# Both heads of an attention job in turn, block by block, with the causal mask added on VectorE

## What is computed

```python
# branch a: 12 query heads of 64 in 4 key groups, window of 128, ALiBi bias, sinks
scores = jnp.where(valid, q @ k.T * d**-0.5 + bias, NEG)        # a block of 128 queries sees 256 keys
m = jnp.maximum(jnp.max(scores), sink)
p = jnp.exp(scores - m);  denom = jnp.sum(p) + jnp.exp(sink - m)
# branch b ("forgetting"): 12 heads of 64, causal over all 512 tokens
sc = q @ k.T * scale + cq[..., None] - c[:, :, None, :]
sc = jnp.where(key_pos <= qpos, sc, NEG);  p = jax.nn.softmax(sc)
# branch c: 4 heads of 128 over 256 memory tokens, no mask
sc = q @ mk.T * d**-0.5;  p = jax.nn.softmax(sc)
out = p @ v                                                      # in all three
```

## Time and profile before

| | |
|---|---|
| median of 3 runs | 2411.13 us |
| profiled execution, span from first to last instruction | 2409.1 us |
| TensorE products busy | 2273.2 us (94%), 10216 instructions |
| TensorE weight loads busy | 1830.8 us (76%) |
| VectorE busy | 1176.2 us (49%) |
| ScalarE busy | 803.9 us (33%) |
| GpSimd busy | 255.5 us (11%) |
| mean granted TensorE clock | 0.975 of full speed |

### The profile page before, as it was taken

The page is one execution under the profiler, slowest core; times in us unless marked ns, Lnnn a source line. Parts: engine busy times, 40 slices in busy tenths (PEclk is TensorE's granted clock), DMA queues, the critical chain, the costliest instruction groups (busy, mean ns, idle before and its releaser), DMA issues.

```text
span 2409.1 us, 32542 instructions
## 1 busy us (share of the span) xinstructions
PE 2273.2 (94%) x10216; PEld 1830.8 (76%) x10216; DVE 1176.2 (49%) x2028; ACT 803.9 (33%) x1515; POOL 255.5 (11%) x243
## 2 busy tenths in 40 slices
PE   3669999989996899999999999999999999999999
PEld 1457888868775777777777778888888888888887
DVE  4985445566766654444455555543333333334432
ACT  3123222233334334444444444522222222223221
POOL 0860000002220121111001011100000000000000
PEclk8789999999997999999999999999999999999999
DMA  8652333355552432222221222233232333332443
GB/s 354 230 224 70 96 96 96 96 184 189 188 198 81 136 118 78 78 78 78 70 79 61 76 65 90 83 98 96 96 96 96 96 97 99 97 97 89 140 149 113
DMA packets 75822, 280.22 MB, mean 116 GB/s; under 512 B 8677, under 2 KB 11493, under 8 KB 68337
## 3 DMA queue, kind: packets, MB, share of 16 engines
q1 hardware_dynamic: 67872, 259.40, 32.7%
q10 hardware_dynamic: 4848, 10.62, 1.1%
q0 software_dynamic: 3040, 9.46, 1.1%
HBM read 269.98 MB, written 9.46 MB: 116 GB/s over the span
## 4 chain that ended last, share of the span: by engine, by line
PE 81%; DVE 6%; issue 4%; DVEq 3%; DMA 3%; ACT 2%; ACTq 1%; SPq 0%; POOL 0%; POOLq 0%
PE bank L361 25%; PE bank L363 24%; PE bank L362 24%; PE bank L451 3%; PE bank L481 2%; DMA x<-x_features 2%; DVE w_lo L355 1%; PE bank L465 1%; ACT w_hi L345 1%; PE bank L489 1%; DMA w_raw<-stream 1%; DVE h_raw L1196 1%; DVE x_lo L1201 1%; DVE wmod L1172 0%; DVE mod L1177 0%
## 5 line engine op out<-in xcount | busy, mean ns | idle before, releaser
L361 PE MATMUL bank<-x_hi,w_hi 128*128 128x512 f32 x2896 | 1158.0, 400 | 71.0 <-DVE x_lo L1201 53.7
L362 PE MATMUL bank<-x_lo,w_hi 128*128 128x512 f32 x2896 | 1133.3, 391 | 0.0
L363 PE MATMUL bank<-x_hi,w_lo 128*128 128x512 f32 x2896 | 1132.8, 391 | 0.0
L355 DVE TENSOR_TENSOR w_lo<-w_raw,w_hi 128x512 fp32r<-128x512 f32 x724 | 507.2, 701 | 1067.8 <-ACT w_hi L345 1041.6
L345 ACT ACTIVATE w_hi<-w_raw 128x512 fp32r<-128x512 f32 x724 | 457.4, 632 | 1194.8 <-PE bank L363 1096.6
L361 PEld LDWEIGHTS bank<-x_hi,w_hi 128*128 128x128 f32 x2896 | 547.3, 189 | 206.8 <-DVE x_lo L1201 55.8
L363 PEld LDWEIGHTS bank<-x_hi,w_lo 128*128 128x128 f32 x2896 | 546.8, 189 | 116.9
L362 PEld LDWEIGHTS bank<-x_lo,w_hi 128*128 128x128 f32 x2896 | 547.4, 189 | 114.8 <-issue 5.7
L733 POOL TENSOR_TENSOR probs<-probs,rden 128x128 f32<-128x128 f32 (+2 forms) x112 | 80.3, 746 | 547.4 <-DVE rden L644 547.4
L549 ACT ACTIVATE probs<-probs,neg_max 128x128 f32<-128x128 f32 (+2 forms) x112 | 57.8, 517 | 90.3 <-DVE neg_max L632 90.0
L1503 POOL TENSOR_TENSOR w_lo<-front_raw,w_hi 128x512 fp32r<-128x512 f32 x32 | 77.6, 2446 | 32.6 <-ACT w_hi L345 32.6
(11 more groups left out here) (146 smaller groups left out, 1254.8 us busy)
## 6 DMA issues: line engine op xcount, KB each, us to landing
w_raw<-stream SPq DMA_DIRECT2D x362, 512.0 KB, 3.8
wmod<-w_mod_rows SPq DMA_DIRECT2D x48, 1024.0 KB, 6.5
front_raw<-stream SPq DMA_DIRECT2D x8, 1024.0 KB, 8.4
x<-x_features ACTq DMA_DIRECT2D x4, 1024.0 KB, 21.5
x_in<-x_features SPq DMA_DIRECT2D x16, 256.0 KB, 6.6
x_store<-tmp POOLq DMA_DIRECT2D x16, 256.0 KB, 3.5
x_back<-x_store SPq DMA_DIRECT2D x16, 256.0 KB, 4.5
result_features<-result ACTq DMA_DIRECT2D x16, 256.0 KB, 4.3
```

The lines of the kernel that those rows point to most:

```text
L355: nc.vector.tensor_tensor(w_lo[:, q, :], raw_quarter(s), w_hi[:, q, :].bitcast(F32), ALU.subtract).then_inc(lo_ready, 1)
L361: nc.tensor.matmul(bank_ap[:, :tokens], hi, x_hi[:, kx, :], start=start, stop=False)
L362: nc.tensor.matmul(bank_ap[:, :tokens], hi, x_lo[:, kx, :], start=False, stop=False)
L363: return nc.tensor.matmul(bank_ap[:, :tokens], lo, x_hi[:, kx, :], start=False, stop=stop)
```

## The change

- The causal mask is no longer a product on TensorE. `causal` is kept as fp32, and `dve_scores` adds it on VectorE to the 128 columns of neg_c that belong to the diagonal of the block, for both heads, before the scores of that block are read. The bf16 identity and mask and their copies at the start go.
- Scores, exponentials, scaling, transposes and values go by a running number k over both heads. `block_of` gives head and block: head k % 2, block k // 2 in a, and the largest block first in b. Banks alternate by k % 2. A pair (2p, 2p + 1) is the same block of both heads.
- Scores of pair p stand before quarter p + 1, transposes of pair p before quarter p + 4 (two heads) or p + 5 (one head, as before). All values of a two-head job stand behind quarter 7, with the heads alternating inside each key block. In c they stay before quarter 7.
- The denominator is made per pair, one beat behind the exponentials. The sink exponential in a is made per block (one column) instead of per head (four columns).

```diff
+                self.pairs = 2 * self.heads
+                self.base = self.head.times(4)
+                self.turn_beat = 4 if self.heads == 2 else 5
+        def block_of(kind, k):
+            if kind == "c":
+                return 0, k
+            return k % 2, NB - 1 - k // 2 if kind == "b" else k // 2
...
+        def pe_scores(pe, at, p):
...
+            for k in (2 * p, 2 * p + 1):
+                slot, n = block_of(at.kind, k)
+                rows, width, k0 = rows_of(at.kind, slot), LEN[at.kind][n], KEY0[at.kind][n]
+                pe.wait_ge(score_read, (at.base + k + ONE).value())
+                nc.tensor.matmul(score[k % 2][:, :width], q_t[rows, n * P:(n + 1) * P],
+                                 k_t[rows, k0:k0 + width], start=True, stop=True).then_inc(score_full, 1)
-                if at.kind == "b":
-                    mm = nc.tensor.matmul(score[n % 2][:, width - P:width], ident_b[:, :], causal_b[:, :],
-                                          start=False, stop=True, skip_group_check=True)
...
+        def pe_turn(pe, at, p):
+            for k in (2 * p, 2 * p + 1):
+                slot, n = block_of(at.kind, k)
+                pe.wait_ge(probs_ready, (at.base + (k + 1)).value())
+                pe.wait_ge(turned_copied, (at.base + k + ONE).value())
...
+        def pe_values(pe, at):
...
+            for p in range(NB):
+                ks = [p] if at.heads == 1 else [2 * p, 2 * p + 1]
+                pe.wait_ge(turned_copied, (at.base + (ks[-1] + 2) + ONE).value())
+                n = block_of(at.kind, ks[0])[1]
                 count = LEN[at.kind][n] // P
                 for kb in range(count):
                     o = OFF[at.kind][n] + kb * P
+                    for slot in range(at.heads):
+                        rows = rows_of(at.kind, slot)
+                        mm = nc.tensor.matmul(ctx_out[rows, n * P:(n + 1) * P], v_n[:, KEY0[at.kind][n] // P + kb, rows],
+                                              probs_t[:, slot, o:o + P], start=kb == 0, stop=kb == count - 1)
...
+            def before(beat):
+                if at and 1 <= beat <= at.pairs:
+                    pe_scores(pe, at, beat - 1)
+                if beat == 2 and w.prev == "v":
                     pe_turn_values(pe, msrc, T, w.misc_n)
+                if at and 0 <= beat - at.turn_beat < at.pairs:
+                    pe_turn(pe, at, beat - at.turn_beat)
+                if beat == 6 and w.first != "gate":
                     pe_squares(pe, msrc, ones if w.first == "qc" else blocks, T, w.misc_n + (w.prev == "v"))
+                if beat == 7 and at and at.kind == "c":
+                    pe_values(pe, at)
...
+            if at and at.kind != "c":
+                pe_values(pe, at)
...
+                if at.kind == "a":
+                    nc.scalar.activation(sink_exp[:, k:k + 1], neg_max[:, k:k + 1], ACT.Exp,
+                                         bias=sink_col[:, slot:slot + 1]).then_inc(sink_done, 1)
...
+                if at and 1 <= s <= at.pairs:
+                    act_exp(act, at, s - 1)
                 if s == 4 and w.first != "gate":
...
+                if at and 0 <= s - at.turn_beat < at.pairs:
+                    act_turned(act, at, s - at.turn_beat)
...
+        def dve_scores(dve, at, p):
             dve.drain()
+            if at.kind == "b":
+                n = block_of("b", 2 * p)[1]
+                for slot in range(2):
+                    if p == 0:
+                        dve.wait_ge(neg_c_loaded[slot], (at.job + 1).times(16).value())
+                    seg = neg_c[:, slot, n * P:(n + 1) * P]
+                    nc.vector.tensor_tensor(seg, seg, causal[:, :], ALU.add)
+                dve.drain()
...
+                if at and 2 <= s < 2 + at.pairs:
+                    dve_denominator(dve, at, s - 2)
+                if at and 1 <= s <= at.pairs:
+                    dve_scores(dve, at, s - 1)
```

More of the change, by code:

```diff
@@ L447, in pe_scores @@
                     pe.wait_ge(k_ready, at.keys.value())
[L448 to L452, removed]
-                if at.kind == "b":
-                    mm = nc.tensor.matmul(score[n % 2][:, width - P:width], ident_b[:, :], causal_b[:, :],
-                                          start=False, stop=True, skip_group_check=True)
-                mm.then_inc(score_full, 1)
@@ L466, in pe_turn @@
                 mm.then_inc(turned_full, 1)
[L468 to L477, removed]
+        def pe_values(pe, at):
+            pe.wait_ge(ctx_free, (at.job + ONE).value())
+            if at.kind == "c":
+                pe.wait_ge(v_loaded, (at.keys.times(16)).value())
+            else:
+                pe.wait_ge(v_ready, at.keys.value())
+            for p in range(NB):
+                ks = [p] if at.heads == 1 else [2 * p, 2 * p + 1]
+                pe.wait_ge(turned_copied, (at.base + (ks[-1] + 2) + ONE).value())
+                n = block_of(at.kind, ks[0])[1]
@@ L536, in pe_window @@
[L536 to L544, removed]
-            for n in (2 * half, 2 * half + 1):
-                c = 4 * slot + n
-                act.wait_ge(score_read, (head.times(4) + (n + 2) + ONE).value())
-                seg = probs[:, slot, OFF[at.kind][n]:OFF[at.kind][n] + LEN[at.kind][n]]
-                nc.scalar.activation(seg, seg, ACT.Exp, bias=neg_max[:, c:c + 1], scale=-1.0,
-                                     accum_out=den[:, c:c + 1]).then_inc(exp_done, 1)
-            if at.kind == "a" and half == 1:
-                nc.scalar.activation(sink_exp[:, 4 * slot:4 * slot + 4], neg_max[:, 4 * slot:4 * slot + 4], ACT.Exp,
-                                     bias=sink_col[:, slot:slot + 1]).then_inc(sink_done, 1)
@@ new lines, in pe_window, with act_exp @@
+            for n in range(2):
+                panel(pe, w.g + n, w.r + n, x1_hi, x1_lo, {q: lambda q=q: before(4 * n + q) for q in range(4)})
+            if at and at.kind != "c":
+                pe_values(pe, at)
+        def act_exp(act, at, p):
+            for k in (2 * p, 2 * p + 1):
+                slot, n = block_of(at.kind, k)
+                act.wait_ge(score_read, (at.base + (k + 2) + ONE).value())
+                seg = probs[:, slot, OFF[at.kind][n]:OFF[at.kind][n] + LEN[at.kind][n]]
+                nc.scalar.activation(seg, seg, ACT.Exp, bias=neg_max[:, k:k + 1], scale=-1.0,
+                                     accum_out=den[:, k:k + 1]).then_inc(exp_done, 1)
+                if at.kind == "a":
+                    nc.scalar.activation(sink_exp[:, k:k + 1], neg_max[:, k:k + 1], ACT.Exp,
+                                         bias=sink_col[:, slot:slot + 1]).then_inc(sink_done, 1)
@@ L558, in act_turned @@
+        def act_turned(act, at, p):
+            if p == 0:
                 act.wait_ge(pv_done, (at.head + ONE).value())
-            for n in (2 * half, 2 * half + 1):
-                act.wait_ge(turned_full, (head.times(4) + (n + 1)).value())
+            for k in (2 * p, 2 * p + 1):
+                slot, n = block_of(at.kind, k)
+                act.wait_ge(turned_full, (at.base + (k + 1)).value())
                 o, width = OFF[at.kind][n], LEN[at.kind][n]
-                nc.scalar.activation(probs_t[:, slot, o:o + width], turned[n % 2][:, :width], ACT.Copy).then_inc(turned_copied, 1)
+                nc.scalar.activation(probs_t[:, slot, o:o + width], turned[k % 2][:, :width], ACT.Copy).then_inc(turned_copied, 1)
@@ L647, in dve_window @@
             at = w.attention
-            two = at is not None and at.heads == 2
             before = acc[(w.r - 1).parity()]
@@ L726, in pool_window @@
             if at:
-                for slot in range(at.heads):
-                    head = at.head + slot
-                    pool.wait_ge(rden_ready, (head + 1).value())
-                    for n in range(NB):
+                for p in range(at.pairs):
+                    pool.wait_ge(rden_ready, (at.head.times(2) + (p + 1)).value())
+                    for k in (2 * p, 2 * p + 1):
+                        slot, n = block_of(at.kind, k)
                         seg = probs[:, slot, OFF[at.kind][n]:OFF[at.kind][n] + LEN[at.kind][n]]
-                        by = rden[:, 4 * slot + n:4 * slot + n + 1].to_broadcast([P, LEN[at.kind][n]])
+                        by = rden[:, k:k + 1].to_broadcast([P, LEN[at.kind][n]])
                         nc.gpsimd.tensor_tensor(seg, seg, by, ALU.mult).then_inc(probs_ready, 1)
```

96 lines of the change are left out of this document (16 added, 80 removed).

## The result

| | before | after |
|---|---|---|
| median | 2410.98 us (4 runs) | 2432.82 us (4 runs, 2430.65 to 2437.58) |
| profiled execution, span | 2409.1 us | 2429.1 us |
| ratio after / before | | 1.0096, 95% interval 1.0084 to 1.0109 |

The account below looks back on a forecast made before the run. TensorE was taken to bound the kernel, nearly all in the panel products. Savings of 9.1, 3.4 and 28.9 us against an 18.6 us wait gave -22.8 us, from 2411.1 to 2388 us, range 2372 to 2415.

Parts of the forecast that it names:

- Mask off TensorE: Score groups of the b windows: dropping the bf16 mask products saves 0.38 us a group, -9.1 us.
- hidden on VectorE: Mask additions in b windows: some 0.9 us per beat with drains and moved reciprocal, within beats of over 4 us.
- One value group: Values of the 12 two-head windows: one group instead of two saves one 0.28 us shape change each, -3.4 us.
- Overlap: Score and value passes on alternating array halves run side by side: 10.9 us from scores, 18 from values, -28.9 us.
- TensorE takes passes strictly in order, A1 A2 B1 B2: Score pairs: B1 could go along with A2, so a pair takes three pass times instead of four.
- the weight loads at 0.05 us: Value passes: that load pace is just what halving needs, so 80% of the halving was taken, 18 us.
- The wait for copies: Beat 5 of two-head windows: TensorE waits for ScalarE's copies of turned blocks, 1.5 us (b) or 1.6 (a), +18.6 us.
- the upper bound of 26 us: Most the wait on ScalarE's copies could cost: 2.2 us a window, with the split slowed by GpSimd.
- My sum for ScalarE at beat 4: Durations counted from quarter 3's end: b copies done at 5.45 and 5.95 us, TensorE asking at 4.42.
- The wait for VectorE's score reads: Beats 3 or 4: no such wait expected, held covered by 0.3 us or more; seeing one would show the forecast wrong.
- Rival 2: Halves run serially and the beat 5 wait on ScalarE's copy is larger, 2.2 us a window: +14, 2425 us; chance 0.11.
- 16.8 to 18.6: Total wait on ScalarE's copies at beat 5, in us: without overlap of the array halves, and with it.

Follow-up runs that it names:

- e7: The kernel before with only the mask moved from TensorE to additions on VectorE (it hides more keys than it should); 2403.11 us, ratio 0.9970.
- e3: The changed kernel with both the early copy of the first turned pair on ScalarE and the late denominator on VectorE; 2367.68 us, ratio 0.9821.
- e2: The changed kernel with VectorE making the denominator behind the score reads of its beat instead of ahead of them; 2399.31 us, ratio 0.9953.
- e4: The changed kernel with three useless fp32 products on TensorE at the start of beat 5 of each two-head window; 2422.91 us, ratio 1.0048.
- e5: On e3, within each query block's values all key blocks of one head come first, then those of the other; 2370.12 us, ratio 0.9833.
- e9: On e3, all value passes of head 0 in the group come first, then all of head 1; 2381.83 us, ratio 0.9879.
- e1: The changed kernel with ScalarE copying the first turned pair at beat 4 ahead of exponentials and norm; 2395.04 us, ratio 0.9935.

## Why the prediction was wrong

The terms for work saved came true or better. The steps that failed are the ones on waiting: the start and so the size of the wait for copies, the wait for score reads put at nothing, and the clock, which has no term.

**Mask off TensorE, -9.1: right.** e7 gives 7.5 us (interval 4.8 to 9.6) for it alone. (0.87 us for 1024 columns is 0.85 ns a column, not 0.83; with it the term is -8.8.) That its additions are "hidden on VectorE" was wrong. 0.29 us each was right for VectorE alone, but beside GpSimd's scaling it was 0.77, and the new place of the denominator brought the two together.

**One value group, -3.4: right** (2.54 us hold one change of shape of 0.36 where there were two of about 0.33).

**Overlap, -28.9: right that it happens, too small.** It is 12.8 + 9.0 us for scores and 13.1 + 9.2 for values, 44 us. The wrong step is "TensorE takes passes strictly in order, A1 A2 B1 B2". Passes for the other half are taken ahead of those that must wait, so a pair takes two pass times and not three, and the weight loads at 0.05 us did not hold the values back. By itself this error would have made the kernel faster than forecast.

**The wait for copies, +18.6: place and cause right, size wrong.** It was 31.3 us, 2.6 us a window, also above the upper bound of 26 us. My sum for ScalarE at beat 4 began at the end of quarter 3. In an a window of the changed kernel quarter 3 ends near 1319.7, but ScalarE is at the last exponentials of beat 3 until 1320.9 and splits at 1321.03:

```profile
1320.62 0.28 ACT L532 ACTIVATE sink_exp<-neg_max,sink_col 128x1 f32<-128x1 f32 x1
1321.03 0.63 ACT L343 ACTIVATE w_hi<-w_raw 128x512 fp32r<-128x512 f32 x1
1321.69 0.69 DVE L353 TENSOR_TENSOR w_lo<-w_raw,w_hi 128x512 fp32r<-128x512 f32 x1 [1.89 <-ACT w_hi L343]
...
1323.38 0.51 ACT L529 ACTIVATE probs<-probs,neg_max 128x256 f32<-128x256 f32 x1 [1.72 <-DVE neg_max L610]
```

Split, split, denominator, score read, exponentials: one beat of this loop between ScalarE and VectorE takes 4.3 us (split to split, 1316.72 to 1321.03), and TensorE's beat had shrunk to 3.6. Some 0.35 us of it is VectorE's split waiting behind the gate's reciprocal, and with the late denominator of e3 this beat takes 3.65 us, so the loop is not a fixed bound. Durations were taken from the trace, but the start from a beat that was longer. In b the additions beside the scaling add up to 1.7 us in a beat.

**The wait for VectorE's score reads, "which I hold to be covered by 0.3 us or more": wrong.** It came 12 times, 17.7 us, from the same additions. In e2 it is 5.4 us.

**Not in the sum at all: the clock, 21 us.** I counted a wait of 1.5 us as 1.5 us. Behind seven of the ten waits of 2.7 to 3.0 us TensorE ran at the 1.2 GHz level, and behind five of the waits of 1.5 to 2.3 us, so the forecast's own wait should have had a price for it too. e4 shows this part by itself. The Trainium skill, "TensorE: Matmul & The Clock Gate", Part 1, says that long idle gaps between bursts of matmuls halve the clock for the burst behind them, and the trace agrees (0.61 over the 4.4 us behind the wait of 2.89 us).

**Sum.** -9.1 - 3.4 - 44 = -56.6 (rounded), waits +49, clock +21: +13, and 7 us that the list of waits does not hold: +20 in the profiled executions, +22 in the medians. Rival 2 had the right direction (slower), but not its reason: its halves were serial, and the wait on ScalarE's copies alone, 31.3 us, is less than the 56.6 us saved. It takes the waits for score reads and the clock as well. The forecast let the overlap lengthen the wait for copies by 1.8 us in all (16.8 to 18.6). No case of mine joined full overlap with losses that outweigh what is saved.

## What to carry to other kernels

When a change shortens a beat of the bounding engine, sum the beat again for each of the others from where they now stand, not from where the bounding engine starts. A loop between two helpers (here 4.3 us) can be longer than the shortened beat (3.6 us). Before moving a step a beat ahead, look at what stands in front of its partner in that partner's own order; here two lines of order (copy first, denominator last) turned +22 us into -43. Give waits of TensorE of 1.5 us and more a second price for the clock: twelve of the waits of the changed kernel had a fall behind them, 21 us in all. And look which instruction of GpSimd an added VectorE operation with two SBUF inputs will stand beside.

## What the runs showed of the hardware

- Passes on the two halves of the array (64 rows, or 64 columns) start 0.006 us apart and run at full pace each: 40 passes of 128 fp32 columns in a record of 2.40 us, as long as that of 20 passes on one half.
- TensorE does not keep matmuls in program order across halves. A pass for the idle half overtakes three or four passes for the busy one (e5: the fifth pass of head 0 runs beside the ninth of the program; e9: the seventeenth beside the twenty-first). This is read from the starts, as the records don't name the half. The Trainium skill, "TensorE: Matmul & The Clock Gate", Part 2, says that only weight loads are pulled ahead and matmuls stay in order; the measurement differs from it.
- A 128x128 fp32 addition on VectorE took 0.29 us alone and up to 1.18 beside a 1.04 us multiplication on GpSimd.
- TensorE's clock fell to the 1.2 GHz level behind waits of 2.7 to 3.0 us (seven of ten), and also behind waits of 1.5 to 2.3 us (five times in the changed kernel). In e1, with no wait over 2.5 us, it fell seven times.
